# Decoder block on one core: nine Strassen pairs in the down projection, their weight sums made ahead

## The reference

```python
merged = g_r * (y_rnn @ w_proj_rnn[l]) + g_a * (y_attn @ w_proj_attn[l])
x = x + gate1[:, None, :] * (merged @ w_out[l])
h = modulate(rmsnorm(x, g_norm2[l]), shift2, scale2)
gf, uf = jnp.split(h @ w_ffn_up[l], 2, axis=-1)
gf = causal_dwconv(gf, w_ffn_conv[l], b_ffn_conv[l])
y_ffn = (jax.nn.gelu(gf, approximate=True) * uf) @ w_ffn_down[l]
x = x + gate2[:, None, :] * y_ffn
...
return modulate(rmsnorm(x, g_final), shift_f, scale_f)
```

## Time and profile before

| | us |
|---|---|
| median of 3 runs | 957.11 (957.03 to 957.27) |
| the profiled execution | 957.39 |
| its span, first to last instruction | 955.6 |
| ScalarE busy | 427.3 (45%) |
| VectorE busy | 655.9 (69%) |
| DMA, mean over the span | 140 GB/s, 133.66 MB |

### The profile page before, as it was taken

One profiled execution on the slowest core, in us unless ns is written; L12 is line 12 of the kernel. 1 busy time (PEld: TensorE's weight loads), 2 busy tenths in 40 slices (PEclk: granted clock), 3 DMA queues, 4 the chain that ended last, 5 costly groups with the idle time before them and its releaser, 6 DMA issues.

```text
span 955.6 us, 12259 instructions
## 1 busy us (share of the span) xinstructions
PE 945.5 (99%) x4638; PEld 801.2 (84%) x4638; DVE 655.9 (69%) x930; ACT 427.3 (45%) x566; POOL 10.3 (1%) x33
## 2 busy tenths in 40 slices
PE   8999999999999999999999999999999999999996
PEld 8888888888988888989888899888888888888885
DVE  4889998522578788863678546777674356789747
ACT  6579777222147253553524474222232223453511
POOL 0120000000000000000000000000000000000000
PEclk9999999999999999999999999999999999999999
DMA  9753312336644535423227503665532523342401
GB/s 330 260 155 99 99 44 72 99 99 196 196 153 157 179 109 200 135 85 108 89 87 253 188 3 123 206 205 190 191 116 89 206 98 103 143 163 101 177 23 66
DMA packets 107378, 133.66 MB, mean 140 GB/s; under 512 B 5324, under 2 KB 81860, under 8 KB 107212
## 3 DMA queue, kind: packets, MB, share of 16 engines
q1 hardware_dynamic: 106952, 132.57, 41.8%
q10 hardware_dynamic: 388, 0.58, 0.2%
HBM read 131.00 MB, written 2.14 MB: 139 GB/s over the span
## 4 chain that ended last, share of the span: by engine, by line
PE 99%; DVE 0%; POOL 0%; DVEq 0%; issue 0%; ACT 0%; POOLq 0%
PE ps L1988 27%; PE ps L1989 27%; PE ps L1990 27%; PE ps L2429 4%; PE ps L2428 4%; PE ps L2427 4%; PE ps L2055 2%; PE ps L2248 1%; PE ps L2038 0%; PE ps L2075 0%; PE ps L2377 0%; PE ps L2047 0%; DVE o_nat L1980 0%; DVE x L1970 0%; DVE x L1972 0%; DVE o_nat L1974 0%
## 5 line engine op out<-in xcount | busy, mean ns | idle before, releaser
L1988 PE MATMUL ps<-h,wsplit 128*128 128x512 f32 (+1 forms) x816 | 312.2, 383 | 0.0
L1990 PE MATMUL ps<-h,wsplit 128*128 128x512 f32 (+1 forms) x816 | 310.8, 381 | 0.0
L1989 PE MATMUL ps<-h,wsplit 128*128 128x512 f32 (+1 forms) x816 | 310.7, 381 | 0.0
L1186 DVE TENSOR_TENSOR wsplit<-wraw,wsplit 128x2048 fp32r<-128x2048 f32 (+2 forms) x77 | 162.3, 2108 | 70.7 <-ACT wsplit L728 70.6
L728 ACT ACTIVATE wsplit<-wraw 128x2048 fp32r<-128x2048 f32 (+2 forms) x77 | 136.2, 1768 | 129.6 <-PE ps L1990 104.2
L1990 PEld LDWEIGHTS ps<-h,wsplit 128*128 128x128 f32 x816 | 153.4, 188 | 29.5
L1988 PEld LDWEIGHTS ps<-h,wsplit 128*128 128x128 f32 x816 | 153.4, 188 | 28.8 <-issue 0.2
L1989 PEld LDWEIGHTS ps<-h,wsplit 128*128 128x128 f32 x816 | 153.5, 188 | 28.5
L1897 DVE SCALAR_TENSOR_TENSOR cv<-ps,vec,cv 128x511 f32<-128x511 f32 (+1 forms) x48 | 35.9, 748 | 49.2 <-ACT cv L1121 46.3
L1243 DVE SCALAR_TENSOR_TENSOR ada_acc<-ada_raw,small,ada_acc 128x512 f32<-128x512 f32 x84 | 63.1, 751 | 2.8
L1121 ACT ACTIVATE cv<-ps,vec 128x512 f32<-128x512 f32 x24 | 18.7, 780 | 98.4 <-PE ps L1990 98.4
(11 more groups left out here) (301 smaller groups left out, 1484.7 us busy)
## 6 DMA issues: line engine op xcount, KB each, us to landing
wraw<-in_w_ffn_up SPq DMA_DIRECT2D x24, 1024.0 KB, 5.2
wraw<-in_w_in SPq DMA_DIRECT2D x23, 1024.0 KB, 5.3
ada_raw<-in_w_ada SPq DMA_DIRECT2D x16, 1024.0 KB, 6.0
wraw<-in_w_ffn_down SPq DMA_DIRECT2D x9, 1024.0 KB, 4.9
ada_raw<-in_w_ada_final SPq DMA_DIRECT2D x8, 1024.0 KB, 5.1
ada_first<-in_w_ada SPq DMA_DIRECT2D x7, 1024.0 KB, 11.8
wraw<-in_w_in SPq DMA_DIRECT2D x12, 512.0 KB, 3.8
wraw<-in_w_proj_rnn SPq DMA_DIRECT2D x8, 640.0 KB, 4.3
```

What stands on the lines that cost most here:

```text
L1186: ve.tensor_tensor(wsplit[:, s, LO, 0:n], wraw[:, s, 0:n], wsplit[:, s, HI, 0:n].bitcast(F), ALU.subtract).then_inc(w_lo, 1)
L1988: te.matmul(dst, lhs(LO), rhs(HI), start=start, stop=False)
L1989: te.matmul(dst, lhs(HI), rhs(LO), start=False, stop=False)
L1990: return te.matmul(dst, lhs(HI), rhs(HI), start=False, stop=stop)
```

## The change

- `NS` goes from 4 to 9: nine pairs and three plain chunks (`N_PLAIN` = 3).
- The sums of the weights are made ahead. For each pair SyncE loads its 1 MB (`sums_load`, two transfers) into one of two slots at 160 and 168 KB, VectorE adds in place (`weight_sums`, four instructions of 128x512), and SyncE stores the result to a DRAM tensor sums_dram (`sums_store`). Five pairs go into the mixer stage, four into up steps 7 to 9. SyncE waits for the sums before each store, and for the stores before it fills a slot again. ScalarE waits for the five stores before it writes vw_hi, which lies over these slots.
- The down stage is one sequence `SEQ` of 21 chunks with a ring of three for raw and split weights and for activations: first parts 0 to 8, plain chunk 0, second parts 0 to 8, plain chunks 1 and 2. The last of these has split places of its own. A first part loads 256 KB of w_ffn_down and 768 KB of sums, a second part 256 KB of sums and 512 KB of weights. `cross_terms(0)` stands on VectorE behind the first of the second parts, `cross_terms(1)` behind all chunks.
- Two chunks instead of three are left for the end, in the order of the last lines of the diff. What VectorE does with a token block is the same; o_nat moves from 80 KB to 128 KB, over x1_nat.

```diff
-NS = 4
-C_PLAIN = C_DOWN + NS - 1
+NS = 9
 N_PLAIN = NF // 2 - NS
-C_END = C_PLAIN + N_PLAIN - 2
+N_END = 2
+N_MIX_SUMS = NS - 4
...
+        SEQ = [("F", p) for p in range(NS)] + [("P", 0)]
+        for p in range(NS):
+            SEQ.append(("Q", p))
+            if p < N_PLAIN - 1 - N_END:
+                SEQ.append(("P", p + 1))
+        SEQ += [("P", m) for m in range(N_PLAIN - N_END, N_PLAIN)]
+        LAST = len(SEQ) - 1
+
+
+        ORDER_HI = [("a", 0), ("a", 1), ("w", 0), ("w", 1)]
+        ORDER_LO = [("a", 0), ("w", 0), ("a", 1), ("w", 1)]
+        for n in range(2, LAST + 1):
+            ORDER_HI += [("w", n), ("a", n)]
+            ORDER_LO += [("w", n), ("a", n)]
...
+        def wait_slot(eng, n):
+
+            if n == 0:
+                eng.wait_ge(w_used, whole(C_DOWN - 2))
+            elif n < 3:
+                eng.wait_ge(w_used, whole(C_DOWN - 1))
+            else:
+                eng.wait_ge(dn_used, n - 2 + (3 if n - 3 >= NS - 1 else 0))
...
+            def sums_load(p):
+
+                if p > 1:
+                    sp.wait_ge(sums_stored, 16 * stores)
+                raw = sums_raw[p % 2][:, :].rearrange("p (k s n) -> p k s n", k=2, s=2)
+                for s in range(2):
+                    sp.dma_start(raw[:, :, s], w_dn_v[:, 2 * p:2 * p + 2, T - T * s:D - T * s])\
+                      .then_inc(sums_loaded[p % 2], 16)
+
+            def sums_store(p):
+                nonlocal stores
+                sp.wait_ge(sums_made, 4 * p + 4)
+                wait_from(sp, sums_stored, 16 * p)
+                stores += 1
+                sp.dma_start(sums_dram[p], sums_raw[p % 2][:, :]).then_inc(sums_stored, 16)
...
+            load_mix(3)
+            load_mix(4)
+            sp.wait_ge(y_part, 16)
+            sums_load(0)
+            sums_load(1)
+            load_mix(5)
+            load_mix(6)
+            load_mix(7)
+            sums_store(0)
+            load_mix(8)
+            sums_load(2)
+            load_mix(9)
+            sums_store(1)
+            load_mix(10)
+            sums_load(3)
+            load_mix(11)
+            sums_store(2)
+            load_mix(12)
+            if N_MIX_SUMS > 4:
+                sums_load(4)
             load(C_MIX + 13, 0, cols_of(w_pr_v, 5 * P, P), NR, P)
+            sums_store(3)
             load(C_MIX + 14, 0, cols_of(w_pr_v, 6 * P, P), NR, P)
+            if N_MIX_SUMS > 4:
+                sums_store(4)
             load(C_MIX + 15, 0, cols_of(w_pr_v, 7 * P, P), NR, P)
             load_ada2(4)
...
             load_up(8)
             sp.wait_ge(ada_out, 7)
...
+            sp.wait_ge(ada_part, 8 * (16 - N_START) + ADA_FIRST)
+            sums_load(N_MIX_SUMS)
+            sums_load(N_MIX_SUMS + 1)
             load_up(9)
-            sp.dma_start(wraw_p2[:, :].rearrange("p (k n) -> p k n", k=2), w_dn_v[:, 4:6, :]).then_inc(pairs_loaded, 16)
+            sums_store(N_MIX_SUMS)
...
+            load_up_half(20)
+            sums_load(N_MIX_SUMS + 2)
+            sums_store(N_MIX_SUMS + 1)
+            load_up_half(21)
+            sums_load(N_MIX_SUMS + 3)
+            load_up_half(22)
+            sums_store(N_MIX_SUMS + 2)
+            load_up_half(23)
+            sums_store(N_MIX_SUMS + 3)
...
+            def load_down(n):
+                kind, p = SEQ[n]
+                raw, loaded = raw_of(n), loaded_of(n)
+                if n < 2:
+                    sp.wait_ge(w_lo, C_DOWN + 1 + n)
+                elif n > 2:
+                    sp.wait_ge(dn_lo, lo_count("w", n - 3))
+                if kind == "F":
+                    sp.dma_start(raw[:, 0:T], w_dn_v[:, 2 * p, 0:T]).then_inc(loaded, 16)
+                    sp.dma_start(raw[:, T:4 * T], sums_dram[p, :, 0:3 * T]).then_inc(loaded, 16)
+                elif kind == "Q":
+                    sp.dma_start(raw[:, T:2 * T], sums_dram[p, :, 3 * T:4 * T]).then_inc(loaded, 16)
+                    sp.dma_start(raw[:, 2 * T:4 * T], w_dn_v[:, 2 * p + 1, :]).then_inc(loaded, 16)
...
+                    tile = 2 * NS + 2 * p
+                    sp.dma_start(raw.rearrange("p (k n) -> p k n", k=2), w_dn_v[:, tile:tile + 2, :])\
+                      .then_inc(loaded, 16)
+            sp.wait_ge(sums_stored, 16 * NS)
+            load_down(2)
+            load_down(0)
+            load_down(1)
+            for n in range(3, LAST + 1):
+                load_down(n)
...
+            def weights_high(n):
+
+                ae.wait_ge(loaded_of(n), load_count(n))
+                if n < LAST:
+                    wait_slot(ae, n)
                 else:
...
             up_step(NF // 2 - 2, lambda i: (hi(C_UP + 2, i), act_high(0)))
             act_high(1)
-            up_step(NF // 2 - 1, lambda i: pair_high(0))
-            pair_high(1)
...
+            def weight_sums(p):
+
+                ve.wait_ge(sums_loaded[p % 2], 32 * (p // 2 + 1))
+                w = [sums_raw[p % 2][:, T * n:T * n + T] for n in range(4)]
+                ve.tensor_tensor(w[1], w[1], w[0], ALU.add).then_inc(sums_made, 1)
+                ve.tensor_tensor(w[0], w[0], w[2], ALU.add).then_inc(sums_made, 1)
+                ve.wait_ge(sums_made, 4 * p + 1)
+                ve.tensor_tensor(w[2], w[1], w[2], ALU.add).then_inc(sums_made, 1)
+                ve.wait_ge(sums_made, 4 * p + 3)
+                ve.tensor_tensor(w[3], w[2], w[3], ALU.add).then_inc(sums_made, 1)
+            for j in range(KD - 3):
                 lo(C_MIX + 4, j, KD * P)
                 gate_product(j, C_MIX + 3, 2, j)
                 lo(C_MIX + 5, j, NR * P)
+                if j < N_MIX_SUMS:
+                    weight_sums(j)
...
+            def act_sums(n):
+
+                kind, p = SEQ[n]
+                x11, x21, x12, x22 = x_of(p)
...
+            def low(n):
+                if SEQ[n][0] != "P":
+                    act_sums(n)
+                weights_low(n)
+                act_low(n)
...
+            up_step(7, lambda i: lo(C_UP + 2, i))
+            weight_sums(N_MIX_SUMS)
+
+            def sums_between(i):
                 lo(C_UP + 2, i)
-                act_lows(0)
-                act_sums(1)
-            up_step(NF // 2 - 2, pairs_between)
+                weight_sums(N_MIX_SUMS + i - 7)
+            up_step(8, sums_between)
+            up_step(9, sums_between)
+            weight_sums(N_MIX_SUMS + 3)
+
+            def sums_first(i):
+                lo(C_UP + 2, i)
+                act_sums(0)
+            up_step(NF // 2 - 2, sums_first)
...
-            def first_pairs(i):
...
+            act_low(0)
+            act_sums(1)
+
+            def first_low(i):
+                weights_low(0)
+                act_low(1)
+            up_step(NF // 2 - 1, first_low)
             act_sums(2)
-            pair_low(1)
-            pair_low(2)
-            act_lows(2)
-            pair_sums(3)
...
-            plain_low(0)
+            weights_low(1)
+            weights_low(2)
+            act_low(2)
+            for n in range(3, NS + 1):
+                low(n)
+            act_sums(NS + 1)
             ve.wait_ge(bc_done, 1)
             cross_read()
-            q_sums(0)
-            plain_low(1)
-            q_lows(0)
+            weights_low(NS + 1)
+            act_low(NS + 1)
             cross_terms(0)
-            q_sums(1)
-            plain_low(2)
-            q_lows(1)
+            for n in range(NS + 2, LAST + 1):
+                low(n)
             cross_terms(1)
...
+            def end_half(n, b, half):
+
+                te.wait_ge(dn_lo, chunk_done(n))
+                for u in range(2):
+                    ins = down_half(n, u, b, half, False, n == LAST and u == 1)
+                if n == LAST:
+                    ins.then_inc(down_mm, 1)
+
+            for n in range(LAST + 1 - N_END, LAST):
+                for b in range(2):
+                    for half in range(2):
+                        end_half(n, b, half)
+            for b in range(2):
                 for half in range(2):
-                    for u in range(2):
-                        down_half((C_END - 1) % 2, u, b, half, False, False)
-                    for n in range(2):
-                        if b == 0 and half == 0:
-                            te.wait_ge(wx_lo, 3 * n + 3)
-                        for u in range(2):
-                            ins = down_half_x(n, u, b, half, n == 1 and u == 1)
-                    ins.then_inc(down_mm, 1)
+                    end_half(LAST, b, half)
+            for b in range(2, NB):
+                for half in range(2):
+                    for n in range(LAST + 1 - N_END, LAST + 1):
+                        end_half(n, b, half)
```

More of the change, by code:

```diff
@@ L421, in upto @@
-        def upto(table, name):
-            names = list(table)
-            return sum(table[n] for n in names[:names.index(name) + 1])
-        RING_OF = {0: C_DOWN, 1: C_DOWN + 1, 3: C_DOWN + 2}
+        SEQ = [("F", p) for p in range(NS)] + [("P", 0)]
[5 more added lines that the diff above has]
+        LAST = len(SEQ) - 1
```

(61 more changed lines are left out.)

410 lines of the change are left out of this document (135 added, 275 removed).

## The result

The changed kernel takes 959.16 us (median of 13 runs, 958.90 to 959.83) against 957.25 us (median of 13, 956.72 to 957.93) for the kernel before: a ratio of 1.002, 95% interval 1.0013 to 1.0028. That is 1.9 us more where 1.7 were forecast, and it lies on the 0.2% up to which the prediction counts a difference as none: the interval does not say on which side. TensorE does 6.8 us less work, and none of it shows in the time.

What follows compares the result with a forecast made beforehand. TensorE, busy 945.5 of 955.6 us, bounded the kernel; its 6.8 us saving would hand the end to VectorE's tail, 954.8 against 953.16 us, so 957.11 + 1.7 = 958.8 us, range 958.0 to 962.0.

Steps and rivals of the forecast that it cites:

- The tail: Kernel end: VectorE works eight halves without a wait, 28.2 us from 926.6 to 954.8 us, against 953.16 before.
- The down stage does not starve: Down stage: VectorE prepares each second part in 3.9 us against TensorE's 4.08, so TensorE never waits; nothing charged.
- The last cross term: Before the tail: VectorE is through the second cross terms at 925.3 us, 1.3 us before the first half is complete.
- The last up step: Up stage, step 11: the last chunk's low part ends at 811.0 us, TensorE wants it at 812.1; covered by 1.1.
- The sum: Whole kernel: the end moves from 953.16 to 954.8 us, +1.7 us, added to the median of 957.11.
- the last matmul: End of the down stage: 30 fewer matmuls, 6.8 us, let it end at 941.35 us if nothing new holds TensorE.
- The chunk's landing: Mixer to attention: first attention chunk lands at 245.9 to 246.1 us, behind the fifth sum's store; needed by about 246.4.
- The hand-over (second rival): Mixer to attention: the fifth sum's store makes the first attention chunk land at 248.5 us, +2.1, 960.9; chance 0.23.
- Starvation (third): Down stage: VectorE, at 95% in nine second parts or late in the tail, costs 1 to 4 us; chance 0.10.
- The gain kept (fourth): Kernel end: VectorE's tail is shorter or overlaps TensorE; 950.3 us if TensorE-bound, 954 for half; chance 0.10.
- That pairs don't save (fifth): Down stage: pairs do not save what they claim, for example by order of products; 957 to 958 us; chance 0.02.

Runs made afterwards that it cites:

- store_twice: The changed kernel with one more 1 MB store behind that of the fifth weight sum: 961.68 us, ratio 1.0050 to the kernel before.
- bare_after: The changed kernel without the sum with x1 and the gain product in VectorE's tail (results wrong, only timed): 950.95 us, ratio 0.9931 to the kernel before.
- light_after: The changed kernel without the gain product in VectorE's tail (results wrong, only timed): 956.01 us, ratio 0.9985 to the kernel before.

## Why the prediction was right

**Right in its mechanism.** The tail: start 926.65 (926.6 forecast), length 28.14 (28.2), end 954.79 (954.8), and no gap after the first product except, in block 0, VectorE's wait for ScalarE, which loads a table for 1.28 us there (930.90 us in its timeline): this block takes 7.75 us against 6.77, the 0.98 that the earlier trace rows gave. The down stage does not starve: VectorE is busy for 41.49 of 49 us in the first parts. Two second parts in a row that nothing holds (their first sums start at 883.56 and 887.42 us) take it 3.86 us each, where 3.9 were forecast; later it goes in step with TensorE, 4.08 us each (the third sum of two successive parts starts at 900.41 and 904.49 us). The last cross term ends at 925.5 us, with 1.2 us of room (1.3 forecast). The last up step: the low part is through at 810.8 us (811.0 forecast, 812.1 allowed). The sum was +1.7 us, the span shows +1.6, the medians +1.9.

**Where it was luck.** That the last matmul ends at 941.34 us, with 941.35 forecast, is in part chance: a gap of 0.24 us, which the sum put at nothing, and a start 0.29 us early cancel. The chunk's landing is another such case. The forecast took 15.2 to 15.4 us from the end of the fifth sum to it, of them 2.6 us "of start", for which no row was given and which no run shows by itself. In the changed kernel the sum ended at 230.29 us, 0.4 earlier than forecast, and the landing came 16.0 us later, since the stream did not run at 388 GB/s throughout (the windows at the end of this document). The two nearly cancel as well.

**The rivals.** The hand-over (second rival) did appear, with a gap of 0.24 us, about a ninth of its price: the chunk was 0.2 us late, and not the 2.1 that the 2.4 us behind the bytes would have made it. store_twice shows that its mechanism is real and its room used up. Starvation (third) is refuted by the windows. The gain kept (fourth) is refuted by the blocks' 6.77 us; bare_after shows what it would have been. That pairs don't save (fifth) is refuted by the last matmul.

**What I had not seen.** The prediction did not ask what one pair less would cost (6 matmuls, 1.36 us, and 1.1 us in the medians) beside what a third chunk at the end gives (5.3 us). And where I priced a step to be left out (light_after), I took it at the independent rate: the term that was mis-sized is 0.61 for 0.73 us, with 0.12 us of the second half on top.

## What to carry to other kernels

Work taken from the busiest engine counts only up to the point where the next engine's serial tail begins: write down when that tail can start, its length when nothing waits, and compare the sum with the end of the busy engine. If the tail is the later one, an arrangement that starts it earlier (here three chunks by token block, not two) is worth more than another saving on the busy engine. Before a queue is given more, ask who waits for the item behind it and how much room it has: here the last of 4.85 MB came 0.2 us too late, and one MB more cost 2.5.

## What the runs showed of the hardware

- VectorE's step after an instruction on which it depends is 0.72 to 0.73 us for 128x512 float32, against 0.60 to 0.61 where it depends on nothing recent. Left out (light_after), such a dependent step gives 0.73 back.
- GpSimd beside VectorE: 128x512 takes GpSimd 1.29 us, and while it runs a VectorE instruction with two inputs in SBUF is held up (1.28 us for 0.69), even one of 128x1 (0.60 for 0.16 us).
- A 1 MB store put ahead of a busy stream of loads delays what is behind it by 2.5 us, no more than its bytes at the stream's 388 GB/s (2.7 us).
- The stream with stores in it is not even. In the changed kernel it moves 262 and 238 GB/s from 232 to 236 us, where the last column was 388 at 232 to 234 us before, and again 382 and 391 from 238 to 242 us. In store_twice, with two such stores in a row, the low stretch comes later. So the dip does not go with the start of a store, and its cause is not shown. The windows of the changed kernel:

```profile
232.00:234.00 2.00, 2.00 (x10) 1.67 (x9) 1.49 (x1) 0.26 (x1) 0.00 (x0) 1.00 1.01 262
234.00:236.00 2.00, 2.00 (x10) 1.65 (x10) 0.00 (x0) 0.00 (x0) 0.00 (x0) 1.00 0.91 238
...
238.00:240.00 2.00, 2.00 (x11) 1.65 (x10) 0.82 (x1) 1.14 (x1) 0.00 (x0) 1.00 1.04 382
240.00:242.00 2.00, 2.00 (x11) 1.65 (x10) 0.67 (x1) 0.00 (x0) 0.00 (x0) 1.00 1.06 391
```

and of store_twice:

```profile
234.00:236.00 2.00, 2.00 (x10) 1.65 (x10) 0.02 (x1) 0.00 (x0) 0.00 (x0) 1.00 1.12 393
236.00:238.00 2.00, 2.00 (x11) 1.65 (x10) 0.50 (x1) 0.00 (x0) 0.00 (x0) 1.00 0.84 185
238.00:240.00 2.00, 2.00 (x11) 1.65 (x10) 0.19 (x1) 0.00 (x0) 0.00 (x0) 1.00 1.14 334
```
